# First norm's row from four per-token roots, and the opening's weight high parts on ScalarE, in a two-layer decoder trunk

## The chip, the cores and the metric

The kernel runs on one core of a Trainium2 chip. The metric is the device time of one execution in microseconds (us). TensorE (PE in the profile) multiplies matrices, VectorE (DVE), ScalarE (ACT) and GpSimd (POOL) work elementwise, and SyncE (SP) issues most transfers from memory (DMA).

## The reference, cut to what matters

Two decoder layers over 512 tokens of width 1024. Only the very beginning is touched by the change: the first RMS norm, the first projection, the convolution behind it, and the norm of the 256 memory tokens.

```python
def rms_norm(x, g):
    xf = xf * lax.rsqrt(jnp.mean(xf * xf, axis=-1, keepdims=True) + NORM_EPS)
    return (xf * g)

# layer 0
hn = rms_norm(h, mix_norm[0])
proj = hn @ w_in                       # 1024 x 3584
x_br, y_br, q, k, v = split(proj)      # 1024, 1024, 512, 512, 512
xc = causal_depthwise_conv(x_br, conv_w, conv_b)   # 4 taps
r = sigmoid(block_diag_linear(xc, wa, ba)); i = sigmoid(block_diag_linear(xc, wx, bx))
# ... recurrence, dilated attention, output projection, then in both layers
h = h + memory_cross_attention(rms_norm(h, xa_norm), rms_norm(mem, xa_mem_norm), ...)
h = h + swiglu(rms_norm(h, ffn_norm), ...)
```

## The kernel before

Features lie on the 128 partitions and tokens along the row, so h is eight tiles of 128x512 (m = 0 to 7). Every float32 matrix is split into a high part that TensorE takes exactly (z_hi, w_hi) and a low remainder (z_lo, w_lo), and each product is made of three: high by high, weight high by z low, weight low by z high.

Weights stream as units of 256 rows by 512 columns (512 KB) into four slots of `raw`, in order: units 0 to 3 and 4 to 7 are the two column groups of the x branch ("in_x", groups 0 and 1), 8 to 11 are q ("in_q"), 12 to 15 the gates. For each unit GpSimd makes w_hi (L706, for unit 0 L724 and L727 in halves), VectorE then makes w_lo (`low_part`, L1455; unit 0 L1466), and TensorE uses both. SP reloads a slot when TensorE has begun the following unit.

The opening (`opening`, unit 0 to 3) goes by row blocks k = 0 to 7, two for each unit: four products w_hi by z_hi (L830), four w_lo by z_hi (L840), four w_hi by z_lo (L843). Tile k of x arrives, ScalarE makes z_hi (L2261) and the square (L2277), VectorE makes z_lo (L1476) and adds the square to `acc` (L1488, L1490). In block 7 `norm_sum` sums `acc` over the partitions: once into every partition (L905), and once for each token into a column (L908). ScalarE takes the root of the full row into `sq` (L2288) and of the columns (L2292), VectorE the reciprocal of the full row, `rstd` (L1535). All later projections wait to be multiplied by `rstd` (`scaled`, L1542).

Behind the opening VectorE's order is written by hand: for each of the eight tiles of the x branch `scaled` into xpad, three taps of the convolution (`conv`, L1689, after ScalarE's first tap L2390), and a low part (`conv_low`, L1697, after ScalarE's high part L2394); between them `low_to` makes the low parts of coming units. Then it scales the four tiles of q (L1542 again). `memory_squares` and `memory_sum` on VectorE (L1558, L1561) add the squares of the memory tokens; TensorE sums them over partitions in the last unit of in_q (`memory_sum`, L916, L918), ScalarE takes the roots (`memory_root`, L2311, L2312), and TensorE begins the four gate groups only after these (s_ms). Group g of products writes the four banks of set g % 2, and begins only when VectorE or ScalarE has read what was there (s_free): the first gate group needs the last x tile scaled, the second needs all four q tiles scaled.

Before the first real product TensorE multiplies ones WARM times (L1100).

Of the kernel before, what the change touches and what calls it, by code (L numbers as in the profile page):

```python
# [29 lines left out]
ALU = mybir.AluOpType  # L30
# [3 lines left out]
P = 128  # L34
# [93 lines left out]
FIRST_TURN = {1: 2, 3: 3, 5: 4, 7: 5}  # L128
WARM = 12
# [61 lines left out]
def trunk(nc, x, mem, w_in, w_gates, w_out0, w_qkv, w_out1, xa_wq, xa_wkv, xa_wo, w_gate_up, w_down,  # L191
          vectors, gains, mask0, mask1, rope_cos, rope_sin, identity, out):
    ctx = ExitStack()
    with ctx:
# [168 lines left out]
        s_raw_first, s_hi_first = sem("s_first_raw_half"), sem("s_first_high_half")  # L363
# [25 lines left out]
        s_rms = sem("s_rms")  # L389
        s_tok_sum, s_tok_rms, s_tok = sem("s_token_sum"), sem("s_token_rms"), sem("s_token_rstd")  # L390
# [121 lines left out]
        def _(sp):  # L512
# [80 lines left out]
            sp.dma_start(raw[:, 0, 0, :], w_in[0:P, 0:512]).then_inc(s_raw_first, 16)  # L593
# [73 lines left out]
        def _(pool):  # L667
# [57 lines left out]
            pool.wait_ge(s_raw[0], 32)  # L725
            pool.sem_inc(s_begun, 1)
            pool.tensor_scalar(w_hi[:, 0, 1], raw[:, 0, 1], 1.0, 1.0, ALU.mult, ALU.mult).then_inc(s_hi, 1)  # L727
            high(1, first + 2)
# [48 lines left out]
        def _(pe):  # L777
# [12 lines left out]
            def group(g_static, g, u0_static, u0, units, rhs, done, n=T, before=None, hook=None, first=0, last=None,  # L790
                      attention_told=False, only=False, hook_at=None):
# [4 lines left out]
                for j in range(first, units if last is None else last):  # L796
# [10 lines left out]
                    for x_, (m, kk) in enumerate(order):  # L807
# [3 lines left out]
                        if hook and (j, x_) == (hook_at or (min(2, units - 1), 4)):  # L811
                            hook()
                        hi, lo = rhs(k)
# [5 lines left out]
            def opening():  # L819

                for k in range(DB):
# [25 lines left out]
            def stage(name, units, rhs, done, ready=None, norm=None, first=0):  # L847
# [6 lines left out]
                if norm == "mix0":  # L854
                    opening()
                else:
                    group(g0, g0, u0, u0, units, rhs, done, before=ready, hook=hook, first=first, only=ng == 1,
                          hook_at={"mem": (3, 4), "ffn1": (2, 5)}.get(norm))
# [4 lines left out]
                if norm == "mix0":  # L863
                    pe.wait_ge(s_tok_rms, 1)
# [22 lines left out]
            def norm_sum(norm, g):  # L887
# [5 lines left out]
                if g >= 2:  # L893
                    pe.wait_ge(s_free[g % 2], free_needed(g))
# [6 lines left out]
                if norm in SPLIT:  # L901
                    pe.matmul(ps[:, bank(g, 3), :], ones_r[:], acc_hi[:], start=True, stop=False)
                    pe.matmul(ps[:, bank(g, 3), :], ones_r[:], acc_lo[:], start=False, stop=True).then_inc(s_sum, 1)
                    return
                pe.matmul(ps[:, bank(g, 3), :], ones[:], acc[:], start=True, stop=True).then_inc(s_sum, 1)  # L905
                if norm == "mix0":
                    for t in range(TB):
                        ins = pe.matmul(ps[:, bank(g, 2), t:t + 1], acc[:, t * P:(t + 1) * P], ones[:, 0:1],  # L908
                                        start=True, stop=True)
                    ins.then_inc(s_tok_sum, 1)  # L910
# [534 lines left out]
        def _(dve):  # L1445
# [17 lines left out]
            def first_low(half):  # L1463

                dve.wait_ge((s_hi_first, s_hi)[half], 1)
# [3 lines left out]
            def residual(norm, done, bias=None, group0=0, norm_next=True, units=(), between=None):  # L1469
# [4 lines left out]
                def low(m):  # L1474
# [3 lines left out]
                    if norm == "mix0" and m in (1, 2):  # L1478
                        if m == 2:
                            summed(1)  # L1480
                            summed(2)
                        return
                    summed(m)
# [214 lines left out]

            for m0_ in (0, 4):
                for i in range(6):  # L1700
# [6 lines left out]
                    if i == 4:  # L1707
                        low_to(UNIT0["in_x"] + m0_ + 9)
# [4 lines left out]
                    low_to(UNIT0["in_x"] + m0_ + {0: 7, 2: 8, 5: 10}.get(i, 0))  # L1713
# [543 lines left out]
        def _(act):  # L2257
            def residual(norm):
# [7 lines left out]
                to_hi = zf_hi if norm[:3] == "ffn" else z_hi  # L2266
                for m in range(DB):
# [5 lines left out]
                    if m >= 2:  # L2273


                        act.wait_ge(s_zl, NORM[norm] * DB + m + (norm == "mix0" and m == 3))
                    act.activation(sq[:, m % 2, :], h[:, m, :], ACT.Square).then_inc(s_sq, 1)  # L2277
                if norm == "mix0":
                    memory_squares()
                if norm in SPLIT:  # L2280
                    act.wait_ge(s_acc, NORM[norm] + 1)
                    act.activation(acc_hi[:], acc[:], ACT.Copy).then_inc(s_ach, 1)
# [541 lines left out]
```

## Time and profile before

| | us |
|---|---|
| median of 3 runs | 1297.3 (1296.27 to 1297.46) |
| the profiled execution | 1297.3 |
| its span in the trace | 1295.5 |
| TensorE busy | 1286.3 (99%) |
| VectorE busy | 921.9 (71%) |
| ScalarE busy | 532.5 (41%) |
| GpSimd busy | 258.7 (20%) |

The profiled execution's own time is 1.8 us above its span and equals the median. TensorE's granted clock is 1.0 of full speed in all slices. A product of 128x512 is listed with some 0.39 us, but they overlap and start about 0.23 us apart.

### The profile page before, as it was taken

How to read it: one execution, taken by the hardware profiler on the slowest of the kernel's cores; microseconds unless marked ns; L12 is line 12 of the kernel's file. 1: busy time of each engine (PE TensorE's matmuls, PEld its weight loads, DVE VectorE, ACT ScalarE, POOL GpSimd, SP SyncE). 2: the span in 40 equal slices, each digit the busy share in tenths (PEclk: the TensorE clock that was granted, in tenths of full speed). 3: DMA queues.
4: the chain of work that ended last, by engine and by line, in shares of the span. 5: the costliest groups of instructions: out<-in, count | busy, mean ns of one | idle time of the engine just before them, and what ended most of it. 6: DMA issues, size and time to landing. Idle time of an engine off the chain costs nothing.

```text
span 1295.5 us, 19991 instructions
## 1 busy us (share of the span) xinstructions
PE 1286.3 (99%) x7554; PEld 1115.4 (86%) x7554; DVE 921.9 (71%) x1458; ACT 532.5 (41%) x1124; POOL 258.7 (20%) x295
## 2 busy tenths in 40 slices
PE   9999999999999999999999999999999999999998
PEld 7778778888888998899988878888888998899986
DVE  8997857446689984388955778557789983489842
ACT  5247356113533560056622347425433550166512
POOL 3111253311422002100021126413321002000010
PEclk9999999999999999999999999999999999999999
DMA  6333323233333333333233332132333323333232
GB/s 236 102 106 113 91 66 98 66 98 98 114 98 98 114 98 98 98 115 98 87 110 114 106 106 69 50 98 88 108 98 98 114 91 94 99 126 98 82 98 98
DMA packets 96701, 130.73 MB, mean 101 GB/s; under 512 B 5312, under 2 KB 61888, under 8 KB 96608
## 3 DMA queue, kind: packets, MB, share of 16 engines
q1 hardware_dynamic: 94976, 127.42, 32.0%
q10 hardware_dynamic: 1632, 2.05, 0.6%
q8 instruction: 60, 0.98, 0.3%
q14 instruction: 33, 0.27, 0.1%
HBM read 124.67 MB, written 2.10 MB: 98 GB/s over the span
## 4 chain that ended last, share of the span: by engine, by line
PE 91%; DVE 5%; issue 2%; DMA 1%; ACT 0%; POOL 0%; SPq 0%; DVEq 0%; POOLq 0%; ACTq 0%
PE ps L784 17%; PE ps L788 16%; PE ps L787 16%; PE ps L942 8%; PE ps L941 8%; PE ps L940 8%; DVE xc L1689 1%; PE ps L1426 1%; PE ps L1427 1%; PE ps L1423 1%; PE ps L1256 1%; PE ps L1272 1%; PE ps L1285 1%; DVE w_lo L1455 1%; PE ps L1145 1%
## 5 line engine op out<-in xcount | busy, mean ns | idle before, releaser
L706 POOL TENSOR_SCALAR w_hi<-raw 128x1024 fp32r<-128x1024 f32 x161 | 184.6, 1147 | 933.9 <-PE ps L942 367.3
L1455 DVE TENSOR_TENSOR w_lo<-raw,w_hi 128x1024 fp32r<-128x1024 f32 x161 | 206.3, 1287 | 178.1 <-POOL w_hi L706 176.2
L784 PE MATMUL ps<-f_hi,w_hi 128*128 128x512 f32 x720 | 281.1, 390 | 1.3 <-ACT small L2312 1.1
L787 PE MATMUL ps<-f_lo,w_hi 128*128 128x512 f32 x720 | 280.2, 389 | 0.0
L788 PE MATMUL ps<-f_hi,w_lo 128*128 128x512 f32 x720 | 280.2, 389 | 0.0
L941 PE MATMUL ps<-zq_lo,quad_hi 128*128 128x256 f32 x896 | 253.6, 283 | 0.0
L940 PE MATMUL ps<-zq_hi,quad_hi 128*128 128x256 f32 x896 | 253.5, 283 | 0.0
L941 PEld LDWEIGHTS ps<-zq_lo,quad_hi 128*128 128x128 f32 x896 | 172.0, 192 | 0.2
L940 PEld LDWEIGHTS ps<-zq_hi,quad_hi 128*128 128x128 f32 x896 | 172.0, 192 | 0.2
L784 PEld LDWEIGHTS ps<-f_hi,w_hi 128*128 128x128 f32 x720 | 135.1, 188 | 30.1 <-ACT small L2312 1.6
L788 PEld LDWEIGHTS ps<-f_hi,w_lo 128*128 128x128 f32 x720 | 135.1, 188 | 28.2
L787 PEld LDWEIGHTS ps<-f_lo,w_hi 128*128 128x128 f32 x720 | 135.2, 188 | 27.7
L942 PE MATMUL ps<-zq_hi,quad_v_lo 128*128 128x256 f32 x512 | 144.9, 283 | 0.0
L784 PE MATMUL ps<-z_hi,w_hi 128*128 128x512 f32 x304 | 120.2, 396 | 0.8 <-DVE w_lo L1455 0.8
L788 PE MATMUL ps<-z_hi,w_lo 128*128 128x512 f32 x304 | 118.4, 390 | 0.0
L787 PE MATMUL ps<-z_lo,w_hi 128*128 128x512 f32 x304 | 118.4, 389 | 0.0
L942 PE MATMUL ps<-zq_hi,quad_raw_lo 128*128 128x256 f32 x384 | 108.7, 283 | 0.0
L2644 ACT ACTIVATE quad_hi<-quad_raw 128x512 fp32r<-128x512 f32 x96 | 57.3, 621 | 114.9 <-DMA quad_raw<-in_w_gate_up 114.1
L942 PEld LDWEIGHTS ps<-zq_hi,quad_v_lo 128*128 128x128 f32 x512 | 98.3, 192 | 0.0
L2086 DVE TENSOR_TENSOR quad_v_lo<-quad_v,quad_hi 128x512 fp32r<-128x512 f32 x128 | 87.7, 688 | 3.0 <-ACT quad_hi L2644 3.0
L2086 DVE TENSOR_TENSOR quad_raw_lo<-quad_raw,quad_hi 128x512 fp32r<-128x512 f32 x96 | 63.9, 686 | 24.2 <-ACT quad_hi L2644 24.0
L2644 ACT ACTIVATE quad_hi<-quad_v 128x512 fp32r<-128x512 f32 x128 | 74.1, 623 | 12.5 <-DVE quad_v L2081 12.4
(267 smaller groups left out, 2042.2 us busy)
## 6 DMA issues: line engine op xcount, KB each, us to landing
quad_raw<-in_w_gate_up SPq DMA_DIRECT2D x64, 512.0 KB
raw<-in_w_down SPq DMA_DIRECT2D x44, 512.0 KB
raw<-in_w_gate_up SPq DMA_DIRECT2D x48, 256.0 KB
raw<-in_w_out SPq DMA_DIRECT2D x20, 512.0 KB
raw<-in_w_in SPq DMA_DIRECT2D x19, 512.0 KB
raw<-in_xa_wkv SPq DMA_DIRECT2D x16, 512.0 KB
raw<-in_w_in SPq DMA_DIRECT2D x18, 256.0 KB, 3.5
raw<-in_xa_wq SPq DMA_DIRECT2D x8, 512.0 KB
```

What stands on the lines that cost most here:

```text
L706: pool.tensor_scalar(w_hi[:, slot], raw[:, slot], 1.0, 1.0, ALU.mult, ALU.mult).then_inc(s_hi, 1)
L784: ins = pe.matmul(o, whi, rhi, start=start, stop=False)
L787: pe.matmul(o, whi, rlo, start=False, stop=False)
L788: return pe.matmul(o, wlo, rhi, start=False, stop=stop)
L940: pe.matmul(o, whi, zh, start=start and k == 0, stop=False, skip_group_check=True)
L941: pe.matmul(o, whi, zl, start=False, stop=False, skip_group_check=True)
L942: ins = pe.matmul(o, wlo, zh, start=False, stop=k == 3, skip_group_check=True)
L1145: ins = pe.matmul(ps[:, mx["s_banks"][e], c0:c0 + P * (i + 1)], q0[r, p, i * P:(i + 1) * P], k0[r, p, 0:P * (i + 1)], start=True, stop=True)
L1256: ins = pe.matmul(ps[:, wn["s_banks"][e], c0:c0 + wn["wide"][i]], q1[r, p, i * P:(i + 1) * P], k1[r, p // 4, P * wn["first"][i]:P * (i + 1 ...
L1455: dve.tensor_tensor(w_lo[:, slot], raw[:, slot], w_hi[:, slot].bitcast(F32), ALU.subtract).then_inc(s_lo, 1)
L2086: dve.tensor_tensor(kind_lo(q, i), kind_full(q, i), kind_hi(i).bitcast(F32), ALU.subtract).then_inc(s_wl, 1)
L2644: act.activation(kind_hi(i), kind_full(q, i), ACT.Copy).then_inc(s_wh, 1)
```

## The change

The first norm no longer takes the root and the reciprocal of the full 128x512 row. `token_sums` sums the squares for each token into columns (128x4), ScalarE takes the root of these, VectorE their reciprocal, then four products of the identity matrix with these columns (128x128 each, into `acc`), and in group 1, after nine products, TensorE multiplies ones by that (`token_rows`), which gives `rstd` in all partitions; ScalarE copies it out. VectorE's memory additions move from right behind the opening to between the fifth and the sixth x tile; ScalarE's memory high parts are spread over the convolution, and the memory roots come before the last convolution tile's high part. The high parts of unit 0's second half and of units 1 to 5 are made by ScalarE (`weight_high`) in place of GpSimd, which makes unit 0's first half in two column halves that arrive by two transfers, one from SP and one from ScalarE's queue. Nine products of ones are made ahead in place of twelve. `low_to` takes other turns.

```diff
-FIRST_TURN = {1: 2, 3: 3, 5: 4, 7: 5}
-WARM = 12
+FIRST_TURN = {1: 2, 3: 3, 5: 4}
+WARM = 9
+FIRST_UNITS = 6
...
-            sp.dma_start(raw[:, 0, 0, :], w_in[0:P, 0:512]).then_inc(s_raw_first, 16)
+            sp.dma_start(raw[:, 0, 0, 0:256], w_in[0:P, 0:256]).then_inc(s_raw_first[0], 16)
...
-            pool.wait_ge(s_raw_first, 16)
-            pool.sem_inc(s_begun, 1)
-            pool.tensor_scalar(w_hi[:, 0, 0], raw[:, 0, 0], 1.0, 1.0, ALU.mult, ALU.mult).then_inc(s_hi_first, 1)
...
-            high(1, first + 2)
+            for side in range(2):
+                c = slice(256 * side, 256 * side + 256)
+                pool.wait_ge(s_raw_first[side], 16)
+                pool.sem_inc(s_begun, 1)
+                pool.tensor_scalar(w_hi[:, 0, 0, c], raw[:, 0, 0, c], 1.0, 1.0, ALU.mult, ALU.mult).then_inc(s_hi_first, 1)
+            pool.wait_ge(s_hi, FIRST_UNITS)
+            high(FIRST_UNITS, first + 2)
...
                     for m in range(4):
+                        if k == 0 and m == 2:
+                            pe.wait_ge(s_hi_first, 2)
...
-                    if k == DB - 1:
-                        norm_sum("mix0", 1)
...
                         pe.matmul(ps[:, m, :], w_lo[:, j, kk, P * m:P * (m + 1)], zh, start=False, stop=False)
+                    if k == DB - 1:
+                        token_sums()
...
+                    group(g0 + 1, g0 + 1, u0 + units, u0 + units, units, rhs, done, hooks={
+                        (0, 3): token_rows, (0, 4): lambda: pe.wait_ge(s_tok_rms, 1),
+                        (0, 6): lambda: pe.wait_ge(s_rms, NORM["mix0"] + 1)})
+                    return
...
+            def token_sums():
+
+                pe.wait_ge(s_acc, NORM["mix0"] + 1)
+                for t in range(TB):
+                    ins = pe.matmul(ps[:, bank(g_sum, 2), t:t + 1], acc[:, t * P:(t + 1) * P], ones[:, 0:1],
+                                    start=True, stop=True)
+                ins.then_inc(s_tok_sum, 1)
+
+            def token_rows():
+
+                pe.wait_ge(s_diag, TB)
+                pe.matmul(ps[:, bank(g_sum, 3), :], ones[:], acc[:], start=True, stop=True).then_inc(s_sum, 1)
...
+                    if not done:
+                        summed(DB - 1)
+                        low_to(5)
...
             residual("mix0", None)
-            memory_squares()
-            one_over_rms("mix0")
-            memory_sum()
             dve.wait_ge(s_tok_rms, 1)
             dve.reciprocal(rms_tok[:, TB:], rms_tok[:, 0:TB]).then_inc(s_tok, 1)
+            dve.wait_ge(s_ident, 16)
+            dve.wait_ge(s_tok, 1)
+            for t in range(TB):
+                dve.tensor_scalar(acc[:, t * P:(t + 1) * P], ident[:], rms_tok[:, TB + t:TB + t + 1], 1.0,
+                                  ALU.mult, ALU.mult).then_inc(s_diag, 1)
+            low_to(UNIT0["in_x"] + 6)
+            dve.wait_ge(s_rms, NORM["mix0"] + 1)
+            dve.nop().then_inc(s_rstd, 1)
...
+            in_turn = {(0, 0): 7, (0, 2): 8, (0, 3): 9, (0, 4): 10, (4, 0): 11, (4, 1): 12, (4, 3): 13}
...
-                    if i == 4:
-                        low_to(UNIT0["in_x"] + m0_ + 9)
+                    low_to(UNIT0["in_x"] + in_turn.get((m0_, i), 0))
+                    if (m0_, i) == (4, 0):
+                        memory_squares()
+                        memory_sum()
...
-                    low_to(UNIT0["in_x"] + m0_ + {0: 7, 2: 8, 5: 10}.get(i, 0))
+            low_to(UNIT0["in_x"] + 14)
...
+            def weight_high(u):
+                act.wait_ge(s_raw[u % SLOTS], 32 * (u // SLOTS + 1))
+                if u == 0:
+                    act.activation(w_hi[:, 0, 1], raw[:, 0, 1], ACT.Copy).then_inc(s_hi, 1)
+                else:
+                    act.activation(w_hi[:, u % SLOTS], raw[:, u % SLOTS], ACT.Copy).then_inc(s_hi, 1)
...
                     high(to_hi, m)
...
+                    if norm == "mix0" and (m % 2 or m == 2):
+                        weight_high({1: 0, 2: 1}.get(m, (m + 1) // 2))
...
+                if norm == "mix0":
+                    act.wait_ge(s_tok_sum, 1)
+                    act.activation(rms_tok[:, 0:TB], ps[:, bank(GROUP0["in_x"] + 1, 2), 0:TB], ACT.Sqrt, bias=v("eps"),
+                                   scale=1.0 / D).then_inc(s_tok_rms, 1)
+                    weight_high(FIRST_UNITS - 1)
+                    act.wait_ge(s_sum, NORM[norm] + 1)
+                    act.activation(rstd[:], ps[:, bank(GROUP0["in_x"] + 1, 3), :], ACT.Copy).then_inc(s_rms, 1)
+                    return
...
+            act.dma_start(raw[:, 0, 0, 256:512], w_in[0:P, 256:512]).then_inc(s_raw_first[1], 16)
...
-            memory_high(0)
...
+                    if m == DB:
+                        memory_root()
                     if i >= 1:
                         act.wait_ge(s_xc, m)
                         act.activation(f_hi[:, m - 1, :], xc[:, m - 1, :], ACT.Copy).then_inc(s_xch, 1)
-            memory_root()
+                        memory_high(0, (m - 1,))
```

How the change moves instructions is seen on two engines. First VectorE, from the end of the opening to its first x tiles, before (xpad is the scaled x tile, mem_sq and mem_rstd are the memory additions; numbers after a name tell buffers apart):

```order
L1455 TENSOR_TENSOR w_lo<-raw,w_hi 128x1024 [waits s_weight_hi]
L1558 TENSOR_TENSOR mem_sq<-mem_sq 128x1024 [waits s_mem_rms]
L1558 TENSOR_TENSOR mem_sq<-mem_sq 128x512 [waits s_dve_chain]
L1535 RECIPROCAL rstd<-sq 128x512 [waits s_rms,s_dve_chain]
L1561 TENSOR_TENSOR mem_rstd<-mem_sq 128x256 [waits s_rstd]
L1684 RECIPROCAL rms_tok<-rms_tok 128x4 [waits s_token_rms]
L1542 TENSOR_TENSOR xpad_79<-ps,rstd 128x512 [waits s_projected_tiles]
L1455 TENSOR_TENSOR w_lo<-raw,w_hi 128x1024 [waits s_dve_chain,s_weight_hi]
L1455 TENSOR_TENSOR w_lo<-raw,w_hi 128x1024 [waits s_weight_hi]
```

and the same place of the changed kernel:

```order
L1469 TENSOR_TENSOR w_lo<-raw,w_hi 128x1024 [waits s_weight_hi]
L1696 RECIPROCAL rms_tok<-rms_tok 128x4 [waits s_token_rms]
L1700 TENSOR_SCALAR acc<-ident,rms_tok 128x128 [waits s_token_rstd,s_ident]
L1700 TENSOR_SCALAR acc<-ident,rms_tok 128x128 x3
L1469 TENSOR_TENSOR w_lo<-raw,w_hi 128x1024 [waits s_weight_hi]
L1557 TENSOR_TENSOR xpad_79<-ps,rstd 128x512 [waits s_rms,s_projected_tiles]
L1469 TENSOR_TENSOR w_lo<-raw,w_hi 128x1024 [waits s_dve_chain,s_weight_hi]
```

The full row's reciprocal is gone, unit 5's low part has come ahead of the first x tile, and the three memory additions have left; they stand further down, between the fifth and the sixth x tile:

```order
L1557 TENSOR_TENSOR xpad_79<-ps,rstd 128x512 [waits s_projected_tiles,s_conv]
L1469 TENSOR_TENSOR w_lo<-raw,w_hi 128x1024 [waits s_dve_chain,s_weight_hi]
L1573 TENSOR_TENSOR mem_sq<-mem_sq 128x1024 [waits s_mem_rms]
L1573 TENSOR_TENSOR mem_sq<-mem_sq 128x512 [waits s_dve_chain]
L1576 TENSOR_TENSOR mem_rstd<-mem_sq 128x256 [waits s_dve_chain]
L1557 TENSOR_TENSOR xpad_80<-ps,rstd 128x512 [waits s_projected_tiles,s_conv]
```

Second ScalarE in the opening, before, from the first tile of x to the fourth (s_x_quarter1 is the arrival of tiles 2 and 3):

```order
L2261 ACTIVATE z_hi<-h,vec 128x512 [waits s_x_quarter0,s_vec]
L2277 ACTIVATE sq<-h 128x512
L2261 ACTIVATE z_hi<-h,vec 128x512 [waits s_x_second_tile]
L2277 ACTIVATE sq<-h 128x512
L2261 ACTIVATE z_hi<-h,vec 128x512 [waits s_x_quarter1]
L2277 ACTIVATE sq<-h 128x512 [waits s_z_lo]
L2261 ACTIVATE z_hi<-h,vec 128x512 [waits s_x_quarter1]
```

and of the changed kernel:

```order
L2291 ACTIVATE z_hi<-h,vec 128x512 [waits s_x_quarter0,s_vec]
L2291 ACTIVATE z_hi<-h,vec 128x512 [waits s_x_second_tile]
L2284 ACTIVATE w_hi<-raw 128x512 [waits s_raw0]
L2300 ACTIVATE sq<-h 128x512
L2291 ACTIVATE z_hi<-h,vec 128x512 [waits s_x_quarter1]
L2286 ACTIVATE w_hi<-raw 128x1024 [waits s_raw1]
L2300 ACTIVATE sq<-h 128x512
L2291 ACTIVATE z_hi<-h,vec 128x512 [waits s_x_quarter1]
L2286 ACTIVATE w_hi<-raw 128x1024 [waits s_raw2]
```

Unit 1's high part now stands behind z_hi of tile 2, so behind the arrival of that part of x, and the square of a tile stands behind the weights.

## Rows read from the trace of the kernel before

**Rows 1.** TensorE's waits, whole span: waiting line <- releaser: us in total, times, longest.

```profile
PE ps L784 <- ACT small L2312: 1.1, 1, 1.1
...
PE ps L784 <- DVE w_lo L1455: 0.8, 1, 0.8
```

**Rows 2.** The chain that ended last, 0 to 200 us: start us, us, what.

```profile
29.94 3.36 DVE rstd L1535
33.32 0.42 DVE mem_rstd L1561
...
75.57 0.63 ACT f_hi L2394
76.20 0.36 ACT mem_rstd L2311
76.77 0.50 PE ps L784
```

**Rows 3.** Timeline 0 to 20 us: start, us, engine line operation [idle before it, releaser].

```profile
1.06 4.52 PE L1100 MATMUL ps<-ones_r 128*128 128x128 f32 x24 [1.06 <-DVE ones_r L1668]
...
5.68 1.20 PE L830 MATMUL ps<-z_hi,w_hi 128*128 128x512 f32 x4
...
9.20 0.72 ACT L2261 ACTIVATE z_hi<-h,vec 128x512 fp32r<-128x512 f32 x1 [2.41 <-DMA h<-in_x]
...
12.18 1.07 PE L840 MATMUL ps<-z_hi,w_lo 128*128 128x512 f32 x4
...
18.03 1.20 PE L840 MATMUL ps<-z_hi,w_lo 128*128 128x512 f32 x4
```

**Rows 4.** Timeline 24 to 37 us, columns as in the group before.

```profile
24.65 2.17 ACT L2304 ACTIVATE mem_sq<-mem_x 128x512 f32<-128x512 f32 x4
24.71 0.75 DVE L1476 SCALAR_TENSOR_TENSOR z_lo<-h,vec,z_hi 128x512 fp32r<-128x512 f32 x1
...
26.33 1.02 PE L905 MATMUL ps<-acc,ones_r 128*128 128x512 f32 x2
...
27.12 2.79 DVE L1558 TENSOR_TENSOR mem_sq<-mem_sq 128x1024 f32<-128x1024 f32 x2
27.18 0.95 PE L908 MATMUL ps<-ones_r,acc 128*128 128x1 f32 x8
...
27.39 0.69 ACT L2288 ACTIVATE sq<-ps,vec 128x512 f32<-128x512 f32 x1 [0.56 <-PE ps L905]
...
29.93 0.40 PE L784 MATMUL ps<-z_hi,w_hi 128*128 128x512 f32 x1
...
33.67 0.17 DVE L1684 RECIPROCAL rms_tok<-rms_tok 128x4 f32<-128x4 f32 x1
33.75 0.66 DVE L1542 TENSOR_TENSOR xpad<-ps,rstd 128x512 f32<-128x512 f32 x1
...
36.36 0.50 PE L784 MATMUL ps<-z_hi,w_hi 128*128 128x512 f32 x1 [0.82 <-DVE w_lo L1455]
```

**Rows 5.** Timeline 55 to 83 us, VectorE and TensorE, columns as before.

```profile
55.33 1.22 DVE L1455 TENSOR_TENSOR w_lo<-raw,w_hi 128x1024 fp32r<-128x1024 f32 x1
...
57.38 1.86 DVE L1455 TENSOR_TENSOR w_lo<-raw,w_hi 128x1024 fp32r<-128x1024 f32 x1 [0.24 <-DVE xpad L1542]
...
68.29 2.60 DVE L1689 SCALAR_TENSOR_TENSOR xc<-xpad,vec,xc 128x512 f32<-128x512 f32 x3 [0.25 <-DVE xpad L1542]
...
71.85 0.59 PE L916 MATMUL ps<-mem_rstd,ones_r 128*128 128x256 f32 x2
...
80.77 0.69 DVE L1542 TENSOR_TENSOR q<-ps,rstd 128x512 f32<-128x512 f32 x1 [0.24 <-DVE q L1542]
...
82.34 0.39 PE L784 MATMUL ps<-f_hi,w_hi 128*128 128x512 f32 x1
```

**Rows 6.** Two lines by themselves: durations in ns, shortest/median/longest, first and last start.

```profile
L1100 PE MATMUL ps<-ones_r x24: 274/421/579, 1.1 to 5.3; 128*128 128x128 f32 x24
L2629 ACT ACTIVATE zq_hi<-zq x14: 1044/1062/1064, 394.8 to 982.3; 128x1024 fp32r<-128x1024 f32 x14
```

More of the change, by code:

```diff
@@ L362, in trunk @@
         s_raw = [sem(f"s_raw{i}") for i in range(SLOTS)]
-        s_raw_first, s_hi_first = sem("s_first_raw_half"), sem("s_first_high_half")
+        s_raw_first = [sem("s_first_raw_left"), sem("s_first_raw_right")]
+        s_hi_first = sem("s_first_high_half")
         s_begun = sem("s_weight_begun")
@@ L790, in group @@
             def group(g_static, g, u0_static, u0, units, rhs, done, n=T, before=None, hook=None, first=0, last=None,
-                      attention_told=False, only=False, hook_at=None):
+                      attention_told=False, only=False, hook_at=None, hooks={}):
                 for j in range(first, units if last is None else last):
@@ L812, in group @@
                             hook()
+                        if (j, x_) in hooks:
+                            hooks[j, x_]()
                         hi, lo = rhs(k)
@@ L855, in stage @@
                     opening()
-                else:
-                    group(g0, g0, u0, u0, units, rhs, done, before=ready, hook=hook, first=first, only=ng == 1,
-                          hook_at={"mem": (3, 4), "ffn1": (2, 5)}.get(norm))
+                    group(g0 + 1, g0 + 1, u0 + units, u0 + units, units, rhs, done, hooks={
+                        (0, 3): token_rows, (0, 4): lambda: pe.wait_ge(s_tok_rms, 1),
+                        (0, 6): lambda: pe.wait_ge(s_rms, NORM["mix0"] + 1)})
+                    return
+                group(g0, g0, u0, u0, units, rhs, done, before=ready, hook=hook, first=first, only=ng == 1,
+                      hook_at={"mem": (3, 4), "ffn1": (2, 5)}.get(norm))
                 if norm == "mem":
@@ L900, in norm_sum @@
                     return
[L901 to L910, printed above, removed]
+                pe.matmul(ps[:, bank(g, 3), :], ones_r[:], acc_hi[:], start=True, stop=False)
+                pe.matmul(ps[:, bank(g, 3), :], ones_r[:], acc_lo[:], start=False, stop=True).then_inc(s_sum, 1)
+            g_sum = GROUP0["in_x"] + 1
+            def token_sums():
[7 more added lines that the diff above has]
+                pe.matmul(ps[:, bank(g_sum, 3), :], ones[:], acc[:], start=True, stop=True).then_inc(s_sum, 1)
             def memory_sum(norm, g):
@@ L1463, in first_low @@
             def first_low(half):
-                dve.wait_ge((s_hi_first, s_hi)[half], 1)
+                dve.wait_ge((s_hi_first, s_hi)[half], (2, 1)[half])
                 dve.tensor_tensor(w_lo[:, 0, half], raw[:, 0, half], w_hi[:, 0, half].bitcast(F32),
@@ L1477, in low @@
                                              ALU.mult, ALU.subtract).then_inc(s_zl, 1)
[L1478 to L1483, printed above, removed]
+                    if norm != "mix0":
+                        summed(m)
+                    elif m:
+                        summed(m - 1)
                 def summed(m):
@@ L2266, in residual, with square @@
                 to_hi = zf_hi if norm[:3] == "ffn" else z_hi
+                def square(m):
+                    if m >= 2:
+                        act.wait_ge(s_zl, NORM[norm] * DB + m + (norm == "mix0"))
+                    act.activation(sq[:, m % 2, :], h[:, m, :], ACT.Square).then_inc(s_sq, 1)
                 for m in range(DB):
@@ L2272, in residual @@
                     high(to_hi, m)
-                    if m >= 2:
-                        act.wait_ge(s_zl, NORM[norm] * DB + m + (norm == "mix0" and m == 3))
-                    act.activation(sq[:, m % 2, :], h[:, m, :], ACT.Square).then_inc(s_sq, 1)
+                    if norm == "mix0" and (m % 2 or m == 2):
+                        weight_high({1: 0, 2: 1}.get(m, (m + 1) // 2))
+                    if norm != "mix0":
+                        square(m)
+                    elif m:
+                        square(m - 1)
+                if norm == "mix0":
+                    square(DB - 1)
                 if norm == "mix0":
@@ L2312, in memory_root, with memory_high @@
                 act.activation(small[:, 2:4], ps[:, b + 1, 0:MB], ACT.Sqrt, bias=v("eps"), scale=1.0 / D).then_inc(s_ms, 1)
-            def memory_high(l):
+            def memory_high(l, tiles=range(DB)):
                 act.wait_ge(s_mem, 16 * (l + 1))
-                for m in range(DB):
+                for m in tiles:
                     act.activation(mem_hi[l][:, m, :], (mem_x0, mem_x1)[l][:, m, :], ACT.Identity,
```

16 lines of the change are left out of this document (4 added, 12 removed).

## The prediction

> **What bounds the kernel now.** I read TensorE's waits first. TensorE is busy for 99% of the span, and only two single waits of the whole execution lie where the change works: 0.8 us for a low part of a weight (w_lo) and 1.1 us for the memory root [rows 1]. Whatever is moved on other engines can be worth no more than what TensorE gets back there, plus what it loses in the opening. The chain of waits says who makes TensorE wait: from the opening to 76.77 us it runs almost wholly over VectorE (rstd's reciprocal of 3.36 us is one link, the last tile's f_hi and the memory root on ScalarE are the end), and then turns to TensorE [rows 2]. So VectorE sets the pace of the first 77 us, and TensorE mostly has enough in hand to hide it.
>
> The timeline gives TensorE's losses by place. Products start 0.2275 us apart: 156 of them lie between 36.36 and 71.85 us [rows 4, 5]. A row block of 12 is thus 2.73 us, a unit of 24 is 5.46 us. (a) The first product starts at 5.68 us [rows 3]. (b) Block 4's weight-low products are due two blocks after block 2's at 12.18, at 17.64, and start at 18.03: with their slow restart some 0.5 us lost [rows 3]. (c) Unit 4 begins at 29.93, so unit 5 is due at 35.39 and begins at 36.36: 0.97 lost, since VectorE makes unit 5's low part only after the reciprocal and the first x tile, 33.75 [rows 4]. (d) The memory sum begins at 71.85 [rows 5]; it takes 0.8 with its columns, and 12 products follow, so the gates are due at 75.4 and begin at 76.77 [rows 2]: 1.4 lost. All this together is about 3.5 us with the start.
>
> **The change part by part.**
>
> *The early start* is worth nothing by my working. Nine products of ones and two column halves let TensorE begin between 5.0 and 5.68 us. But unit 1's high part now stands on ScalarE behind z_hi of tile 2, which waits for x until 9.20 and takes 0.72 [rows 3]. ScalarE's price for 128x1024 isn't shown on this line; zq_hi, a 128x1024 split of the same types, takes 1.06 [rows 6], and I take that (bounds 0.72 for half the width and twice that). Then VectorE's w_lo, 1.22 where nothing runs beside it [rows 5]. Sum: 9.20 + 0.72 + 1.06 + 1.22 = 12.20, against 12.18 for the same products before [rows 3]. From 5.1 us TensorE would be there after 28 products at 11.5, so it waits 0.7 for the low part. The gain of the start is given back at block 2.
>
> *Unit 2's low part* (b). ScalarE has room behind unit 1's (a square, a z_hi and unit 2's high part, 0.6 to 1.1 each, until some 13.2), and VectorE does two z_lo and two sums of at most 0.75 each [rows 4] and then w_lo: 12.2 + 3.0 + 1.2 = 16.4, before 17.64. The 0.5 us of (b) is gained; the later low parts come further ahead.
>
> *The row sum* (L905) leaves the opening and returns in group 1: 27.18 - 26.33 = 0.85 both times [rows 4], no change in sum. The token sums stay: from their start to unit 4's, with 8 products behind them, is 29.93 - 27.18 = 2.75, that is 0.93 for them [rows 4]. After: block 7's weight-low products at 12.2 + 5 x 2.73 = 25.85, token sums at 26.75, four products more, unit 4 at 28.6 against 29.93.
>
> *The diagonal.* ScalarE's root of the columns is ready when its memory squares are done (2.17 us behind the last square [rows 4], which my count puts at 25) and the token sums have ended: about 27.9. VectorE: reciprocal 0.17 [rows 4], then four 128x128 products. None is in the trace; each lies between that 0.17 and the 0.66 of a full 128x512 tile [rows 4]; I take 0.2. The diagonal is ready between 28.8 and 30.8, and TensorE asks for it after nine products of unit 4, at 30.65: at the upper bound it would wait 0.2. The row is then read by ScalarE: the copy starts 1.06 after the sum (27.39 against 26.33) and takes 0.69 [rows 4]. So 30.65 + 1.06 + 0.69: the first x tile is scaled at 32.4 against 33.75, 1.35 earlier. Unit 5's low part is made before that, so (c) is gained: unit 5 begins at 28.6 + 5.46 + 0.85 = 34.9 against 36.36, 1.45 earlier.
>
> *Memory work later.* From the first x tile to the end of q's scaling at 80.77 + 0.69 = 81.46 VectorE is busy without a pause worth naming. In that stretch the change takes out one w_lo, 1.22 [rows 5], and puts in the three memory additions, before 2.79 [rows 4] plus 0.42 [rows 2] = 3.2. The 2.79 had GpSimd's high part of unit 6 beside it; what that costs a two-input operation is seen at w_lo, 1.86 beside one and 1.22 alone [rows 5], so alone they are about 2.5. GpSimd still makes as many high parts in this stretch, so I take 2.5 and count its drag once. q's scaling then ends at 81.46 - 1.35 - 1.2 + 2.5 = 81.4.
>
> *The memory root* (d). Conv tile 6 ends at 70.89 [rows 5]; with as many w_lo ahead of it as before, it ends at 70.9 - 1.35 + 2.5 = 72.0. ScalarE then makes f_hi, a memory high part and the root, 0.6, 0.5 and (76.77 - 76.20) 0.6 [rows 2]: 73.7. TensorE finishes in_q at 75.4 - 1.45 = 73.95. So (d) is gained too, and the first gate group starts at 74.0, 2.8 earlier.
>
> *Where it is given back.* The second gate group writes the banks that q's scaling reads. Before, q was done at 81.46 and the group began at 82.34 [rows 5], with 0.9 in hand. Now TensorE is there at 74.0 + 5.5 = 79.5 and q is done at 81.4: it waits 1.9 us and begins at 81.5. Net gain 0.85 us. Behind this TensorE sets the pace again (ScalarE reads each gate group when it is done, 5.46 us apart), and the gain is carried to the end.
>
> **The sum** against the profiled execution's 1297.3 (its span 1295.5 and 1.8 around it, equal to the median): 1297.3 - 0.9 = 1296.4. Of about 3 us that TensorE's losses offer, VectorE's total work lets through less than 1. Taking 0.2% (2.6 us) as what a measurement of this kernel can tell from no change, this is no change.
>
> **Rivals.**
>
> *VectorE's stretch is shorter than I count, and the whole gain stays.* If q ends by 79.5, TensorE keeps its 2.8 us: 1294.5. It would need VectorE to save 1.9 us more; for it speaks that nine high parts of GpSimd fall into the stretch, each worth up to 0.64 [rows 5], and at other places they may hit operations that don't mind. Against it: their number is unchanged.
>
> *VectorE's backlog grows.* If GpSimd's high part meets the memory additions as it did before, they cost 3.2: q ends at 82.1, and the group starts 0.15 earlier than before: 1297.1. GpSimd Engine Reference, section 1, of the Trainium skill says that GpSimd's SBUF interfaces are shared with VectorE and contend with instructions of two SBUF inputs; the memory additions are all of that kind, while scaling from the product banks has one such input. The trace agrees, 1.86 against 1.22 [rows 5]. If besides x arrives late, so that the first x tile is scaled no earlier than 33.75, q ends at 83.4 and the group at 83.5: 1298.5. It turns to a loss once q ends past 82.3.
>
> *Slower: the first products run at a slower pace.* The ones products show 421 ns at the median and 274 at the shortest [rows 6], while the granted clock reads 1.0 (2.4 GHz) throughout; the real ones from 5.68 on run at full pace [rows 3]. Nine instead of twelve, and a start 0.6 earlier, might put real products into the slow part. Each would cost 0.2 more; TensorE has 0.7 us in hand before block 2, so from the fourth on it is a loss, and a loss of 2.6 us needs some 16 of them, more than a block: 1299.9. TensorE: Matmul & The Clock Gate, part 1, of the Trainium skill states that the array starts throttled to half rate and that activity releases it; by that rule the nine are only worth what they keep busy, and a gap behind them would count against them. No row here shows a fall after a gap.
>
> *The change doesn't do what it says:* the opening ends no earlier, since x sets it. That is the case of the late x above, without the drag: 33.75 and q at 82.8 give +0.5, 1297.8.
>
> **How the numbers follow.** VectorE decides at q, gain 0.2 to 1.9: 0.60. Whole gain kept: 0.15, and 0.02 of the first at its edge: faster by over 0.2%, 0.17. Backlog or late x, 1297.1 to 1298.5: 0.16. Slow first products or a wait I have not seen: 0.09, slower, and 0.01 from the backlog. No change: 0.73. The likeliest is 1296.4. The range takes in the whole gain at 1294.4 and the backlog to 1298.3.
>
> **What the changed profile would show.** Right: block 2's weight-low products near 12.2 behind a wait for w_lo, none at block 4; unit 4 near 28.6; L924's row sum near 30.7 without a wait; first x tile scaled near 32.4; unit 5 with no wait; no wait for the memory root; a new wait of about 2 us of the second gate group for VectorE's scaling of q, near 79.5 to 81.5. Wrong: no wait there (then the gain is whole), a wait for the diagonal, or ones and first products at a lower clock.

## The result and the profile after

The changed kernel takes 1299.37 us (median of 22 runs, 1298.65 to 1300.67) against 1297.28 of the kernel before (22 runs): the ratio is 1.0016, 95% interval 1.0011 to 1.0022. It is slower by 2.1 us, under the 0.2% that I called no change and outside my range (1294.4 to 1298.3). The profiled execution has a span of 1297.7, 2.2 more than before. All of it is lost before 90 us: the second gate group begins 2.0 later, the first scores of the attention 2.1 later, and next to nothing is gained or lost behind them. The chain that ended last has the scores (start us, us, what), before and after:

```profile
142.34 0.86 PE ps L1145 x8
```

```profile
144.48 0.86 PE ps L1159 x8
```

The timeline of the changed kernel at the opening (start, us, engine line operation, idle before it and its releaser):

```profile
9.96 0.72 ACT L2291 ACTIVATE z_hi<-h,vec 128x512 fp32r<-128x512 f32 x1 [1.56 <-DMA h<-in_x]
...
13.02 1.20 PE L845 MATMUL ps<-z_hi,w_lo 128*128 128x512 f32 x4
...
29.22 0.88 DVE L1700 TENSOR_SCALAR acc<-ident,rms_tok 128x128 f32<-128x128 f32 x4
...
29.50 0.39 PE L787 MATMUL ps<-z_hi,w_hi 128*128 128x512 f32 x1
...
31.56 1.02 PE L924 MATMUL ps<-acc,ones_r 128*128 128x512 f32 x2
...
33.36 0.69 DVE L1557 TENSOR_TENSOR xpad<-ps,rstd 128x512 f32<-128x512 f32 x1 [2.12 <-ACT rstd L2327]
```

Against [rows 3, 4]: z_hi of x tile 2, for which ScalarE waits on the transfer, begins at 9.96 instead of 9.20, block 2's weight-low products began at 13.02 instead of 12.18, unit 4 at 29.50 instead of 29.93, and the first x tile was scaled only 0.39 earlier. The four products of the diagonal cost what I took, 0.2 each, and TensorE doesn't wait for them.

The timeline where the time goes, against [rows 5]:

```profile
34.29 1.66 DVE L1469 TENSOR_TENSOR w_lo<-raw,w_hi 128x1024 fp32r<-128x1024 f32 x1 [0.24 <-DVE xpad L1557]
...
45.52 1.06 POOL L709 TENSOR_SCALAR w_hi<-raw 128x1024 fp32r<-128x1024 f32 x1 [3.29 <-DMA raw<-in_w_in]
...
45.78 1.86 DVE L1469 TENSOR_TENSOR w_lo<-raw,w_hi 128x1024 fp32r<-128x1024 f32 x1 [0.25 <-DVE xpad L1557]
...
50.40 1.22 DVE L1469 TENSOR_TENSOR w_lo<-raw,w_hi 128x1024 fp32r<-128x1024 f32 x1
...
51.03 1.50 POOL L709 TENSOR_SCALAR w_hi<-raw 128x1024 fp32r<-128x1024 f32 x1 [4.46 <-DMA raw<-in_w_in]
...
51.53 3.10 DVE L1709 SCALAR_TENSOR_TENSOR xc<-xpad,vec,xc 128x512 f32<-128x512 f32 x3
...
56.87 1.76 DVE L1469 TENSOR_TENSOR w_lo<-raw,w_hi 128x1024 fp32r<-128x1024 f32 x1 [0.24 <-DVE xpad L1557]
...
61.79 1.91 DVE L1469 TENSOR_TENSOR w_lo<-raw,w_hi 128x1024 fp32r<-128x1024 f32 x1 [0.24 <-DVE xpad L1557]
...
72.49 2.98 DVE L1709 SCALAR_TENSOR_TENSOR xc<-xpad,vec,xc 128x512 f32<-128x512 f32 x3
...
75.50 0.63 ACT L2438 ACTIVATE f_hi<-xc 128x512 fp32r<-128x512 f32 x1 [3.40 <-DVE xc L1709]
...
76.44 0.45 ACT L2353 ACTIVATE mem_rstd<-ps,vec 128x256 f32<-128x256 f32 x1
...
77.10 0.50 PE L787 MATMUL ps<-f_hi,w_hi 128*128 128x512 f32 x1 [1.93 <-ACT small L2354]
...
83.54 0.69 DVE L1557 TENSOR_TENSOR q<-ps,rstd 128x512 f32<-128x512 f32 x1 [0.24 <-DVE q L1557]
...
84.34 0.19 PEld L787 LDWEIGHTS ps<-f_hi,w_hi 128*128 128x128 f32 x1 [0.28 <-DVEq L1558]
```

Where a high part of GpSimd holds them up, a w_lo takes 1.66 to 1.91 (1.22 at 50.40, which begins ahead of GpSimd's) and a convolution tile of three operations 3.0 to 3.1 (2.33 undisturbed). Conv tile 6 (72.49) ends late, so f_hi, the root behind it and the gates are late. The scaling of q's last tile ends at 84.23 instead of 81.46, 2.8 later. TensorE waits 1.9 us for the memory root, though it finishes in_q earlier (its last product starts at 74.78, before at 75.25), and the second gate group begins at 84.34 instead of 82.34. VectorE's groups from the first x tile to the end of q (busy us, mean ns of one | idle before), first of the kernel before, then of the changed one:

```profile
L1689 DVE SCALAR_TENSOR_TENSOR xc<-xpad,vec,xc 128x512 f32<-128x512 f32 x24 | 20.2, 842 | 2.0 <-DVE xpad L1542 1.5
L1455 DVE TENSOR_TENSOR w_lo<-raw,w_hi 128x1024 fp32r<-128x1024 f32 x9 | 11.9, 1336 | 0.5 <-DVE xpad L1542 0.5
```

```profile
L1709 DVE SCALAR_TENSOR_TENSOR xc<-xpad,vec,xc 128x512 f32<-128x512 f32 x24 | 20.9, 870 | 1.1 <-DVE xpad L1557 0.5
L1469 DVE TENSOR_TENSOR w_lo<-raw,w_hi 128x1024 fp32r<-128x1024 f32 x8 | 12.1, 1510 | 1.5 <-DVE xpad L1557 1.5
...
L1573 DVE TENSOR_TENSOR mem_sq<-mem_sq 128x1024 f32<-128x1024 f32 (+1 forms) x2 | 1.9, 951 | 0.0
L1576 DVE TENSOR_TENSOR mem_rstd<-mem_sq 128x256 f32<-128x256 f32 x1 | 0.4, 424 | 0.0
```

One w_lo was taken out, and the eight that are left take longer in sum than the nine did. The stretch grew from 47.7 (33.75 to 81.46) to 50.9 us (33.36 to 84.23): 2.3 for the memory additions, 0.2 for w_lo, 0.7 for the convolution. And one thing that I hadn't counted on, in TensorE's row by stretches (window: length, PE busy, PEld, DVE, ACT, POOL, PEclk, DMA share, GB/s):

```profile
77.00:78.00 1.00, 0.90 (x4) 0.77 (x5) 0.96 (x2) 0.04 (x1) 0.00 (x0) 1.00 0.00 0
78.00:79.00 1.00, 1.00 (x4) 0.76 (x3) 0.91 (x2) 0.66 (x2) 0.00 (x0) 0.54 0.24 14
79.00:80.00 1.00, 1.00 (x4) 0.80 (x3) 1.00 (x2) 0.98 (x2) 0.00 (x0) 0.50 0.91 307
...
81.00:82.00 1.00, 1.00 (x4) 0.77 (x4) 0.75 (x2) 0.00 (x0) 0.63 (x1) 0.75 0.09 16
```

Behind the wait for the root the granted clock falls to 0.50 (1.2 GHz), from 78.1 to 81.5 us, and products start 0.43 apart instead of 0.23.

### The profile page after: what moved, and what is told of

Read it like the earlier page. It is cut to its first block, busy times and chain, and to the rows that moved or that the text cites. A ratio compares the mean times of both kernels' runs of the same rounds, so it can differ in the third digit from the quotient of the medians.

```text
span 1297.7 us, 19976 instructions
## 1 busy us (share of the span) xinstructions
PE 1288.3 (99%) x7548; PEld 1116.5 (86%) x7548; DVE 916.5 (71%) x1461; ACT 537.3 (41%) x1130; POOL 252.1 (19%) x290
## 4 chain that ended last, share of the span: by engine, by line
PE 94%; DVE 3%; DMA 1%; ACT 0%; issue 0%; SPq 0%; DVEq 0%; ACTq 0%
PE ps L787 17%; PE ps L790 17%; PE ps L791 17%; PE ps L955 8%; PE ps L956 8%; PE ps L954 8%; PE ps L1440 1%; PE ps L1441 1%; PE ps L1437 1%; DVE xc L1709 1%; PE ps L1270 1%; PE ps L1286 1%; PE ps L1299 1%; DVE w_lo L1469 1%; PE ps L1159 1%; PE ps L1190 1%
## 5 line engine op out<-in xcount | busy, mean ns | idle before, releaser
L709 POOL TENSOR_SCALAR w_hi<-raw 128x1024 fp32r<-128x1024 f32 x156 | 179.3, 1150 | 943.7 <-PE ps L956 368.0
```

The costliest lines, as they stand in the source:

```text
L709: pool.tensor_scalar(w_hi[:, slot], raw[:, slot], 1.0, 1.0, ALU.mult, ALU.mult).then_inc(s_hi, 1)
```

## The experiments

Two theories. Q: VectorE's queue is the loss; q is scaled late, and TensorE needs q's banks for the second gate group. R: the longer wait for the memory root and the slow clock behind it are the loss. Each kernel ran with the kernel before on the same chip (its medians 1297.3 to 1297.5); the ratio is to that, worked out from the single runs, so that it can differ a little from that of the two medians (by 0.0005 at most, in the kernel with the root late).

**The root ahead.** ScalarE's root of the memory norm one place earlier.

```diff
-                    if m == DB:
+                    if m == DB - 1:
                         memory_root()
```

> The changed kernel with ScalarE's memory root one place earlier, ahead of f_hi of conv tile 6 instead of behind it. Theory Q (VectorE's queue sets the second gate group, because q is scaled only at 84.2): the first gate group starts at 75.2 without a wait and runs at full pace, is done at 80.7, and the second then waits 3.6 us and still begins at 84.3; the time stays at 1299.4, within 0.4; 1301 if the clock falls behind the new, longer wait. Theory R (the wait for the root and the stretch at half pace behind it are the loss): the second group begins at 80.7 and 2 to 3.6 us come back, 1295.8 to 1297.3.

Measured: 1302.58, ratio 1.0038 (1.0025 to 1.0052). R falls: the wait for the root is gone, and the time grows, past the 1301 that Q gave for a fall of the clock too. The wait has moved to q, and the slow clock with it:

```profile
79.57 2.07 DVE L1469 TENSOR_TENSOR w_lo<-raw,w_hi 128x1024 fp32r<-128x1024 f32 x1
...
85.15 0.80 PE L787 MATMUL ps<-f_hi,w_hi 128*128 128x512 f32 x1 [4.70 <-DVEq L1558]
```

TensorE waits 4.7 us, and the clock stands at 0.50 from 84 to 90 us, so that the products between 85.15 and 90 lose some 2.4. The w_lo ahead of q now met a high part of GpSimd, 2.07 instead of 1.22, so q ended 0.8 later. The two and the 1299.4 of the changed kernel make 1302.6.

**The additions in the pause.** VectorE waits 3.5 us for the token roots (25.4 to 28.9).

```diff
             residual("mix0", None)
+            memory_squares()
+            memory_sum()
             dve.wait_ge(s_tok_rms, 1)
...
-                    if (m0_, i) == (4, 0):
-                        memory_squares()
-                        memory_sum()
```

> The changed kernel with the memory additions and the memory sum's operand made in VectorE's pause of 3.5 us behind unit 4's low part (25.4 to 28.9), instead of behind the fifth x tile. Theory Q: VectorE's stretch is shorter by the 2.4 us that they take at 58.6 to 60.9; q is scaled at 81.9, the root is no longer waited for, the second gate group begins at 82.0: 1297.0, within 0.5. Theory R: with the root on time 3.6 us come back, 1295.8. If VectorE's delay is something else, 1299.4.

Measured: 1295.98, ratio 0.9991 (0.9982 to 1.0000), 3.4 below the changed kernel. That is less time than Q gave and lies in R's range, so the number doesn't decide between them; the trace does. The root isn't waited for, and the second gate group still begins only when q has ended:

```profile
80.97 0.50 PE L787 MATMUL ps<-f_hi,w_hi 128*128 128x512 f32 x1 [0.96 <-DVEq L1558]
```

The additions lie at 25.18 to 27.59 and delay nothing; q ends at 80.85, 3.4 earlier, of which 2.3 are the additions, 0.45 an earlier x (33.36 to 32.91 for the first tile, in these two profiles), and the rest fewer meetings with GpSimd, less a pause of 0.4 ahead of a w_lo.

**The first block in one transfer.**

```diff
-            sp.dma_start(raw[:, 0, 0, 0:256], w_in[0:P, 0:256]).then_inc(s_raw_first[0], 16)
+            sp.dma_start(raw[:, 0, 0, :], w_in[0:P, 0:512]).then_inc(s_raw_first[0], 16)
...
-                pool.wait_ge(s_raw_first[side], 16)
+                pool.wait_ge(s_raw_first[0], 16)
...
-            act.dma_start(raw[:, 0, 0, 256:512], w_in[0:P, 256:512]).then_inc(s_raw_first[1], 16)
```

> The changed kernel with the first weight block in one transfer of 128x512 on SyncE's queue again, GpSimd's two halves kept. Theory X (the two halves on two queues delay x): ScalarE starts x tile 2 at 9.2 instead of 9.96, block 2's weight-low products at 12.2 instead of 13.0, the first x tile is scaled at 32.6 and q at 83.5: 1298.6, within 0.3. If x is late for another reason, or if the start of VectorE's stretch doesn't carry through, 1299.4.

Measured: 1299.04, ratio 1.0014 (1.0005 to 1.0023), between the two forecasts. In the profiled run z_hi of x tile 2 began at 8.98 and the span was 0.9 shorter, but the medians differ by 0.3 only. Over all profiles z_hi of tile 2 begins between 9.10 and 9.96 with the split (seven), between 9.16 and 9.69 with the transfers of the kernel before (four), and between 8.98 and 9.15 with the change and one transfer (three). It moves by half a microsecond and more between runs of the same transfers, and how much the split adds stays open. What it sets is clear: in every kernel with the change's opening the first x tile is scaled 23.4 us behind z_hi of tile 2 (23.39 to 23.45 in ten profiles).

**High parts by ScalarE.** Units 6 to 14 as well, in nine gaps of its queue, for example:

```diff
                         act.activation(xc[:, m, :], xpad[m % 2][:, 0:T], ACT.Identity, bias=v("conv_b", m),
                                        scale=v("conv_w", m)).then_inc(s_c0, 1)
+                        if m in (0, 4, 5, 6):
+                            weight_high({0: 7, 4: 11, 5: 12, 6: 13}[m])
```

> The changed kernel with the high parts of units 6 to 14 made by ScalarE too, which is idle for much of that stretch; GpSimd begins at unit 15. Theory Q with contention (GpSimd's high parts slow eight of VectorE's two-input operations by 5.2 us in sum, 2.1 more than before): these run at their undisturbed 1.22 and 2.33, q is scaled before 80.7, no wait for the root, the second gate group begins at 80.7, set by TensorE: 1295.7, within 0.5. If ScalarE's copies slow VectorE just as much, or if the operations are slow for another reason: 1299.4.

Measured: 1295.28, ratio 0.9987 (0.9978 to 0.9996). VectorE's groups in the same stretch, from its first x tile to the end of q:

```profile
L1710 DVE SCALAR_TENSOR_TENSOR xc<-xpad,vec,xc 128x512 f32<-128x512 f32 x24 | 18.0, 751 | 1.1 <-DVE xpad L1558 0.5
L1470 DVE TENSOR_TENSOR w_lo<-raw,w_hi 128x1024 fp32r<-128x1024 f32 x8 | 9.8, 1225 | 2.9 <-ACT w_hi L2287 1.7 <-DVE xpad L1558 1.2
```

Without GpSimd beside it every w_lo takes 1.23 and every convolution tile 2.33. Set against these, GpSimd's drag (what its high parts add to VectorE's operations) was 5.2 us in the changed kernel (2.9 on the convolution, 2.3 on the w_lo), and 3.1 before (2.2 and 0.9): 2.1 more, with the same eight high parts. ScalarE's copies, which now run beside the same operations, drag nothing. q ends at 79.76 and TensorE waits 0.3 for it.

**q's banks one by one**, with the root ahead.

```diff
...
-                        if g_static >= 2:
+                        if g_static >= 2 and not by_bank:
...
+                        if by_bank and kk == 0:
+                            pe.wait_ge(s_free[g_static % 2], 4 * (g_static // 2) - 3 + m)
...
-                      before=lambda k: pe.wait_ge(s_xcl, 2 * hd + k + 1))
+                      before=lambda k: pe.wait_ge(s_xcl, 2 * hd + k + 1), only=hd == 1, by_bank=hd == 1)
...
```

> The changed kernel with the root ahead (as in the run before) and the second gate group waiting for q's four banks one by one, its products bank by bank, instead of for all four at once. VectorE's and ScalarE's work is untouched. Theory Q: TensorE is done with the first group at 80.5 and needs only q's first tile, scaled at 81.4 (82.2 if the weight-low ahead meets a high part again): the second group begins 2.0 to 2.8 earlier than in the changed kernel: 1297.0, within 0.6, if its clock stays; 1.7 more if the wait of 1 to 1.7 us brings it down. If something else than q's banks held the group, 1302.6 as with the root ahead alone.

Measured: 1299.23, ratio 1.0012 (1.0004 to 1.0021). Neither 1297.0 nor 1302.6. It lies near the 1298.7 that a fall of the clock would have given, but not for that reason: the clock of the profiled execution stayed at 1.0. The second group did begin at 82.53, 1.8 earlier than in the changed kernel, but TensorE then stood again:

```profile
82.53 0.47 PE L787 MATMUL ps<-f_hi,w_hi 128*128 128x512 f32 x1 [1.89 <-DVEq L1560]
...
89.69 0.50 PE L787 MATMUL ps<-f_hi,w_hi 128*128 128x512 f32 x1 [1.46 <-ACTq L2468]
```

The third group waits for ScalarE to read the first group's banks, and its sigmoids stand behind four gathers of q on ScalarE's queue, the last of which waits for q's last tile. So q's end held TensorE twice.

**The gathers behind the first sigmoids**, on top of the last one.

```diff
-            qk_gathered(0, q0)
             for hd in range(LRU_HEADS):
+                if hd == 1:
+                    qk_gathered(0, q0)
```

> The kernel with q's banks taken one by one, and besides ScalarE's four gathers of q placed behind the first gate group's sigmoids instead of ahead of them. Theory Q, widened (q's late end held TensorE a second time: the gathers wait for q's last tile on ScalarE's queue, the sigmoids that free the first group's banks stand behind them, so the third gate group waited 1.5 us): the third group starts without a wait at 88.1, and 1.5 us come back, 1297.7. If the sigmoids are held by something else: 1299.2.

Measured: 1298.33, ratio 1.0007 (0.9998 to 1.0016), 0.9 of the expected 1.5. The third group's wait is gone; the six executions with a mean clock of 0.999 and 1.0 took 1297.3 to 1298.3, those with 0.997 and 0.998 took 1298.6 to 1299.9.

**The kernel before with the root ahead.**

```diff
+                    if m == DB - 1:
+                        memory_root()
...
-            memory_root()
             act.wait_ge(s_sp_e, 1)
```

> The kernel before with nothing changed but ScalarE's memory root, put ahead of f_hi of conv tile 6. By my prediction's step (d): TensorE's wait of 1.1 for the root goes, the first gate group starts at 75.5 and is done at 80.95, q is scaled at 81.46 as before, and the second group begins at 81.5 instead of 82.34: 0.8 of 1.3 us is kept, 1296.5. If the clock falls behind this wait of 0.5 us: 1298. If the gates were held by something else: 1297.3.

Measured: 1296.53, ratio 0.9993 (0.9984 to 1.0002): as expected, though the interval includes 1, so that the time alone doesn't tell it from no change. In the trace the wait for the root is gone, and TensorE's only wait behind that for the ones is for q, 0.49 us, at 80.68.

**The kernel before with the root late.**

```diff
+            for i in range(2):
+                act.activation(sq[:, i, :], xc[:, DB - 1, :], ACT.Copy)
             memory_root()
```

> The kernel before with two copies of 128x512 to scratch ahead of ScalarE's memory root, so that TensorE waits for it 2.2 us instead of 1.1 (the copies are extra work, nothing reads them). Theory C (a wait of about 2 us brings the granted clock down for some 3.4 us, 1.7 us of products): the first group starts at 77.9, runs half of its products at half pace, and is done at 85.0; 0.9 of the delay is in hand: 1297.3 + 1.1 + 1.7 = 1300.1. If the wait alone counts and the clock stays: 1298.4.

Measured: 1299.93, ratio 1.0014 (1.0005 to 1.0023). It goes by the clock: six executions with a mean clock of 0.998 took 1299.9 to 1300.3 (mean 1300.1), five with 0.999 or 1.0 took 1298.2 to 1298.6 (mean 1298.4). So both numbers of the expectation occur, and the slow clock costs 1.7 us. The wait of the profiled execution and the stretch behind it:

```profile
77.98 0.80 PE L784 MATMUL ps<-f_hi,w_hi 128*128 128x512 f32 x1 [2.09 <-ACT small L2312]
```

```profile
79.00:80.00 1.00, 1.00 (x4) 0.81 (x3) 0.69 (x1) 0.44 (x2) 0.00 (x0) 0.50 0.10 31
```

**The kernel before with the additions later**, the move alone.

```diff
-            memory_squares()
             one_over_rms("mix0")
-            memory_sum()
...
+                    if (m0_, i) == (4, 0):
+                        memory_squares()
+                        memory_sum()
```

> The kernel before with only the memory additions moved to where the changed kernel has them, behind the fifth x tile. Theory Q: they leave the place ahead of rstd's reciprocal, where they held it for 1.8 us and the first x tile for 0.3 more, so the first x tile is scaled at about 31.6; then they return with 2.4 in the same queue, and q's end stays within 0.7 of 81.5, the time at 1297.5, within 0.7. So by themselves they gain and lose as much; only where another edit has already made the reciprocal go (as in the changed kernel, where they would fit into a pause) is the move a plain loss. If the place of the additions is the whole loss of the changed kernel, wherever it comes from: 1299.7.

Measured: 1300.88, ratio 1.0025 (1.0013 to 1.0036). My number missed by 3.4, and the rival's 1299.7, though nearer, was passed too: by itself the move costs the kernel before 3.5 us, so it doesn't gain and lose as much. The gain at the start came as expected, the return cost 4.2 instead of 2.4, since the additions (2.68 instead of 1.95), the convolution and a low part of it (1.53 instead of 0.68) met GpSimd, whose drag was thus some 5.0 against 3.1. And TensorE again waited for the root with the slow clock behind it:

```profile
31.57 0.66 DVE L1542 TENSOR_TENSOR xpad<-ps,rstd 128x512 f32<-128x512 f32 x1
...
55.64 2.68 DVE L1558 TENSOR_TENSOR mem_sq<-mem_sq 128x1024 f32<-128x1024 f32 x2 [0.24 <-DVE xpad L1542]
...
82.81 0.69 DVE L1542 TENSOR_TENSOR q<-ps,rstd 128x512 f32<-128x512 f32 x1 [0.24 <-DVE q L1542]
```

```profile
78.80 0.50 PE L784 MATMUL ps<-f_hi,w_hi 128*128 128x512 f32 x1 [2.48 <-ACT small L2313]
```

**Twelve products of ones** in place of nine, in the changed kernel.

```diff
-WARM = 9
+WARM = 12
```

> The changed kernel with 12 products of ones again instead of 9. By my prediction's first step the start is worth nothing, since x's second quarter sets block 2: the first x tile is scaled 23.4 us behind z_hi of tile 2 whatever the start: 1299.4, within 0.3. If the early start matters, or the first products run slower behind fewer products of ones: 0.3 to 1.0 to one side.

Measured: 1299.35, ratio 1.0015 (1.0006 to 1.0024). The start is worth nothing, as the prediction's first step said.

**Three edits together**: the diffs of the additions in the pause, the high parts by ScalarE and the one first transfer.

> The changed kernel with three of the single edits together: the memory additions in VectorE's pause, units 6 to 14's high parts on ScalarE, the first block in one transfer. Theory Q: VectorE has q scaled by about 77.5, long before TensorE is done with the first gate group, so that TensorE has no wait from block 2 to the gates and sets the time by itself: second group at 79.3 to 79.6, 1295.0, within 0.4; against 79.87 and 1295.3 for the high parts alone, so little is left for the other two. If each edit's gain adds up instead, 1291.9.

Measured: 1294.64, ratio 0.9980 (0.9971 to 0.9989), 4.7 below the changed kernel and 2.8 below the kernel before: it beats both. TensorE's waits of the first 144 us are down to the one for the ones:

```profile
PE ps L1115 <- DVE ones_r L1684: 1.1, 1, 1.1
```

**The three edits and twelve products of ones**, the diff as above.

> The kernel with the three edits together (1294.6, TensorE without a wait up to the gates) and 12 products of ones instead of 9. If TensorE sets the time from its first product on, the start is 0.3 to 0.6 later and so is the end: 1295.1. If x still sets it at block 2: 1294.6.

Measured: 1294.77, ratio 0.9980 (0.9971 to 0.9989). No difference; even here the start isn't what sets the end.

## Why the prediction was wrong

**The steps that held.** The early start is worth nothing. The diagonal (0.2 each), the row sum without a wait, the gain at block 4 and at unit 5, and VectorE as the engine that decides at q's last tile: as written. The opening came out 23.4 us behind z_hi of tile 2, against 23.2 by my count.

**x.** I took tile 2's arrival at 9.20 from one profile. With the split transfer it ranges over 0.9 us (9.10 to 9.96), and the change hangs the whole opening on it. In the profiled execution that is 0.8 of the 0.96 us by which the first x tile came after my 32.4.

**The step that failed** is "memory work later": "GpSimd still makes as many high parts in this stretch, so I take 2.5 and count its drag once." The number of high parts is unchanged, as I said; what they cost isn't. In the kernel before, of the eight ahead of q's scaling, two slowed a w_lo, one met the scaling of an x tile, which reads a product bank and lost nothing (0.69 at 62.44), and the rest met convolution tiles. After the change four slowed a w_lo and four a convolution tile. I forecast +1.3 for the stretch (2.5 added, 1.2 taken out); it was +3.2: 2.3 of additions, less 1.2, and 2.1 of added drag, which I had put at nothing. The w_lo taken out gave nothing back, because the eight left were slowed by 1.4 us more. With these 1.9 and the late x, q ended 2.8 after my 81.4, the second gate group began at 84.34 instead of 81.5, and my own sum with that 2.8 gives 1299.2. The late x alone isn't the cause: with z_hi of tile 2 at 8.98 (the first block in one transfer) q still ended at 83.42, past the 82.3 from which on I had called it a loss.

Nor is the drag a chance of one execution: it is 5 to 6 us in the six profiles of kernels with the order of the change, and about 3 in the three with the order before. The place of the additions makes part of it: moved alone in the kernel before, they bring it from 3.1 to some 5.0; taken back into the pause, from 5.2 to 4.1. What brings the rest, the new turns of `low_to` or another of the moves, no run separates. The high parts by ScalarE show that the drag decides, and the additions in the pause show the rest: the diagonal had just opened a pause of 3.5 us where the additions had stood, and the change moved them out of it into a queue without one.

**The memory root** was to be done at 73.7 and was done at 77.0, when in_q had long ended. Conv tile 6, behind whose high parts it stands, ended at 75.47 instead of 72.0: 0.96 from the late start, 2.7 from GpSimd's drag, which up to there was that much more than before, less 0.2 because the additions took 2.3 and not 2.5. (The 0.5 that I took for a memory high part stands in no row that I named for it; it measured 0.49.)

**The rivals.** "VectorE's backlog grows" was the nearest, but not for the reasons that it gave, and its bound was too low: I let the additions cost 3.2 and the first x tile come no earlier than before (1298.5), and left the other operations' drag as it was. In the profile the additions met no high part (2.3), the first x tile was 0.39 earlier, and the backlog came from those other operations. "The first products run at a slower pace" looked for the slow clock at the start; it stands behind the waits at the gates. In the changed kernel it costs nothing beside q: executions with a mean clock of 0.998 take 1299.35 in the mean (12 runs), with 0.999 they take 1299.44 (5), with 1.0 1299.27 (5), since the second gate group, slow clock or not, waits for q: its first weight load stands 0.28 us for it.

On what GpSimd does to VectorE, SBUF — State Buffer, section "SBUF: two separate sides", of the Trainium skill says that a VectorE instruction with two SBUF inputs and a GpSimd instruction that reads SBUF lock a shared pair of ports against each other, and the one that comes second waits until the other is done. The rows agree to within 0.2: at 45.52 GpSimd begins first and keeps its 1.06, and w_lo, begun 0.26 later, takes 1.86 (1.22 and the 0.80 that GpSimd still needed would be 2.02); at 51.03 GpSimd comes 0.63 behind a w_lo and takes 1.50 (1.06 and the 0.59 that w_lo still needed would be 1.65).

## What to carry to other kernels

Where one engine's queue has no pause, count what its neighbour costs it by which operations meet, not by how many do; better, give that work to an engine that doesn't disturb it. When an edit opens a pause, look at what could stay in it before moving that work away. Of a bound, ask every queue that waits for the same event: q's last tile held TensorE through the banks, and through ScalarE's gathers once the banks were solved.

## What the runs showed of the hardware

A single wait of TensorE can bring its clock to 1.2 GHz. The granted clock stayed at 1.0 behind waits of 0.5 to 1.5 us, fell to 0.50 behind 1.9 (the changed kernel), 2.0, 2.1 (two kernels) and 2.5, and already during 4.7, and stayed up behind 1.9 and 2.0 in two profiled executions with q's banks taken one by one. It is not the same in each execution of one kernel: with a wait of 2.1 us six of eleven executions lost 1.7 us to it. TensorE: Matmul & The Clock Gate, part 1, of the Trainium skill calls the slow start variable from run to run; here the fall behind a wait is, too.
